# Half-height score matmuls in pairs: two heads' index and local-attention scores on the two row halves of the array

## The reference, cut to what matters

```
rel = relu(einsum('bqhd,bsd->bqhs', iq, ik))          # h = 8 heads, d = 64
score = einsum('bqhs,bqh->bqs', rel, iw) * idx_scale  # then the 128 largest
```

```
s = einsum('bnqhgd,bnkhd->bnhgqk', qb, kk)            # d = 64
s = where(mask, s + bias, -inf)
m = maximum(max(s), sink);  p = exp(s - m)
p = p / (sum(p) + exp(sink - m));  o = einsum('bnhgqk,bnkhd->bnqhgd', p, vv)
```

## Time and profile before

| | us |
|---|---|
| median of 3 runs (lowest, highest) | 1807.93 (1806.48, 1810.0) |
| span of the profiled execution, first to last instruction | 1813.4 |
| PE busy in it | 1714.0 (95%) |
| DVE, ACT, POOL busy | 790.4, 698.9, 643.8 |

### The profile page before, as it was taken

One profiled execution on the slowest core, in us unless ns is written; L12 is line 12 of the kernel. 1 busy time (PEld: TensorE's weight loads), 2 busy tenths in 40 slices (PEclk: granted clock), 3 DMA queues, 4 the chain that ended last, 5 costly groups with the idle time before them and its releaser, 6 DMA issues.

```text
span 1813.4 us, 22601 instructions
## 1 busy us (share of the span) xinstructions
PE 1714.0 (95%) x7710; PEld 1362.5 (75%) x7710; DVE 790.4 (44%) x1293; ACT 698.9 (39%) x1133; POOL 643.8 (36%) x269
## 2 busy tenths in 40 slices
PE   5999886999999999999999999889999999999997
PEld 3686663666678888888888788678986877887875
DVE  5486788444423321212123442534323464364464
ACT  4421455344433342323233332753354433243332
POOL 3232231122134444444444342024632344344342
PEclk8998997999999999999999999889999999999998
DMA  4121121111132222232322232013421223222221
GB/s 164 61 82 64 53 75 52 47 46 36 46 116 97 100 94 94 93 103 93 104 93 101 70 100 75 1 47 117 133 99 47 91 84 103 93 93 98 88 93 58
DMA packets 45147, 149.79 MB, mean 83 GB/s; under 512 B 4664, under 2 KB 7872, under 8 KB 45088
## 3 DMA queue, kind: packets, MB, share of 16 engines
q1 hardware_dynamic: 38016, 138.43, 22.9%
q10 hardware_dynamic: 7072, 10.57, 1.7%
HBM read 146.74 MB, written 2.11 MB: 82 GB/s over the span
## 4 chain that ended last, share of the span: by engine, by line
PE 76%; DVE 10%; ACT 7%; issue 5%; DMA 1%; ACTq 1%; DVEq 0%
PE job L304 21%; PE job L306 20%; PE job L305 20%; DVE arena L1317 5%; DVE arena L1320 2%; PE o L491 2%; ACT w_hi L791 2%; ACT arena L1265 2%; PE score L455 2%; PE turn L341 1%; PE score L388 1%; PE score L428 1%; PE score L712 1%; PE o L329 1%; PE job L744 1%
## 5 line engine op out<-in xcount | busy, mean ns | idle before, releaser
L274 POOL TENSOR_TENSOR w_lo<-w_raw,w_hi 128x1024 fp32r<-128x1024 f32 x264 | 643.1, 2439 | 1140.2 <-ACT w_hi L791 1139.8
L304 PE MATMUL job<-a_hi,w_hi 128*128 128x512 f32 (+1 forms) x1144 | 448.1, 392 | 23.7 <-POOL w_lo L274 12.1
L305 PE MATMUL job<-a_lo,w_hi 128*128 128x512 f32 (+1 forms) x1144 | 436.2, 381 | 0.0
L306 PE MATMUL job<-a_hi,w_lo 128*128 128x512 f32 (+1 forms) x1144 | 436.2, 381 | 0.0
L791 ACT ACTIVATE w_hi<-w_raw 128x1024 fp32r<-128x1024 f32 x264 | 275.2, 1050 | 283.3 <-PE job L306 279.8
L304 PE MATMUL job<-b_hi,w_hi 128*128 128x512 f32 x952 | 378.7, 398 | 1.1 <-DVE arena L1320 0.8
L306 PE MATMUL job<-b_hi,w_lo 128*128 128x512 f32 x952 | 371.2, 390 | 0.0
L305 PE MATMUL job<-b_lo,w_hi 128*128 128x512 f32 x952 | 370.7, 389 | 0.0
L304 PEld LDWEIGHTS job<-a_hi,w_hi 128*128 128x128 f32 x1144 | 218.4, 191 | 74.1 <-issue 18.1
L305 PEld LDWEIGHTS job<-a_lo,w_hi 128*128 128x128 f32 x1144 | 218.4, 191 | 41.6 <-issue 2.3
L306 PEld LDWEIGHTS job<-a_hi,w_lo 128*128 128x128 f32 x1144 | 217.9, 190 | 41.4
(11 more groups left out here) (245 smaller groups left out, 1399.3 us busy)
## 6 DMA issues: line engine op xcount, KB each, us to landing
w_raw<-w_all SPq DMA_DIRECT2D x264, 512.0 KB, 3.2
arena<-x_t ACTq DMA_DIRECT2D x8, 512.0 KB, 6.6
out_t<-arena ACTq DMA_DIRECT2D x8, 256.0 KB, 2.0
arena<-rg_w ACTq DMA_DIRECT2D x4, 256.0 KB, 2.7
arena<-row_table ACTq DMA_DIRECT2D x1, 1024.0 KB, 5.0
arena<-mem_t ACTq DMA_DIRECT2D x1, 1024.0 KB, 5.8
arena<-consts ACTq DMA_DIRECT2D x1, 384.0 KB, 4.1
cst<-consts ACTq DMA_DIRECT2D x1, 258.0 KB, 8.6
```

The lines of the kernel that those rows point to most:

```text
L274: nc.gpsimd.tensor_tensor(w_lo[:, sl], raw[:, sl], w_hi[:, sl].bitcast(F32), ALU.subtract).then_inc(s("lo_ready"), 1)
L304: mm(ps[:, 0:n], w_hi[:, sl, c], hi[:, kt, 0:n], start=kt == 0, stop=False)
L305: mm(ps[:, 0:n], w_hi[:, sl, c], lo[:, kt, 0:n], start=False, stop=False)
L306: ins = mm(ps[:, 0:n], w_lo[:, sl, c], hi[:, kt, 0:n], start=False, stop=kt == last)
```

## The change

The zero-padded keys go. `ik_rows` is one tile with the index key in partitions 0 to 63 and the same key in 64 to 127; `s_k` is one tile with the two local key heads one below the other. Each score matmul is issued on the 64 partitions of its own head only, with 64-row weights, which places it on the lower or the upper 64 rows of the array. The two memsets of the padded tiles, and one of two key copies, are gone. In the local-attention stage the blocks of heads 2t and 2t+1 are issued in turn: `swa_scores(0)` makes both heads before the first spreads, and the pair for heads 2t+2 and 2t+3 is issued after the turn of the odd head 2t+1, where before each head's scores came after the turn of the head two before it. The wait on `swa_s` is for both heads of the pair before.

```
-                mm(s_ps[n % 3][:, 0:P * (t + 1)], p1[:, J_IQ + h // 2, t * P:t * P + P],
-                   ikz[:, h % 2, 0:P * (t + 1)], start=True, stop=True).then_inc(s("idx_mm"), 1)
+                r = slice(64 * (h % 2), 64 * (h % 2) + 64)
+                mm(s_ps[n % 3][:, 0:P * (t + 1)], p1[r, J_IQ + h // 2, t * P:t * P + P],
+                   ik_rows[r, 0:P * (t + 1)], start=True, stop=True).then_inc(s("idx_mm"), 1)
...
-            def swa_scores(n):
-                t, half = n // 2, n % 2
-                if n >= 2:
-                    pe.wait_ge(s("swa_s"), n - 1)
+            def swa_block(n, b):
+                t, half = n // 2, n % 2
+                r = slice(64 * half, 64 * half + 64)
+                k0 = max(b - 1, 0) * P
+                c0 = b % 2 * 256 + (P if b == 0 else 0)
+                return mm(banks[half][b // 2][:, c0:b % 2 * 256 + 256], in2[r, 13 + t, b * P:b * P + P],
+                          s_k[r, k0:(b + 1) * P], start=True, stop=True)
+
+            def swa_scores(t):
+
+                if t >= 1:
+                    pe.wait_ge(s("swa_s"), 2 * t)
                 for b in range(QT):
-                    k0 = max(b - 1, 0) * P
-                    c0 = b % 2 * 256 + (P if b == 0 else 0)
-                    ins = mm(banks[n % 2][b // 2][:, c0:b % 2 * 256 + 256], in2[:, 13 + t, b * P:b * P + P],
-                             s_kz[:, half, k0:(b + 1) * P], start=True, stop=True)
+                    ins = swa_block(2 * t, b)
+                    if b == QT - 1:
+                        ins.then_inc(s("swa_mm"), 1)
+                    ins = swa_block(2 * t + 1, b)
                 ins.then_inc(s("swa_mm"), 1)
...
             go_spread(0)
             go_spread(1)
-            swa_scores(1)
...
-                if n < 6:
-                    swa_scores(n + 2)
+                if half == 1 and n < 6:
+                    swa_scores(t + 1)
                 pe.wait_ge(s("swa_pt"), 2 * n + 2)
...
-            did(v.memset(ikz, 0.0))
             dve.wait_ge(s("zeroed"), 1)
             norm_inverse(0)
...
             dve.wait_ge(s("go_ready"), 4)
-            did(v.memset(s_kz, 0.0))
-            settle()
-            did(v.tensor_copy(s_kz[0:64, 0, :], in2[0:64, 17, :]))
-            v.tensor_copy(s_kz[64:128, 1, :], in2[64:128, 17, :]).then_inc(s("swa_keys"), 1)
+            dve.wait_ge(s("job_taken"), J_IN2 + 18)
+            v.tensor_copy(s_k, in2[:, 17, :]).then_inc(s("swa_keys"), 1)
```

More of the change, by code:

```diff
@@ L160, in build @@
         keep = flat(tiles(28, 2)).bitcast(BF16).rearrange("p (t c) -> p t c", c=T)
-        ikz = tiles(30, 2)
+        ik_rows = arena[:, 30, :]
         rel = tiles(32, 2)
@@ L199, in build @@
         g_o = tiles(23, 4)
-        s_kz = tiles(2, 2)
+        s_k = arena[:, 2, :]
         s_vz = tiles(17, 2).rearrange("p g (t c) -> p g t c", c=P)
@@ L857, in _ @@
             act.wait_ge(s("ik_normed"), 1)
-            act.dma_start(ikz[64:128, 1, :], ikz[0:64, 0, :]).then_inc(s("ik_landed"), 16)
+            act.dma_start(ik_rows[64:128, :], ik_rows[0:64, :]).then_inc(s("ik_landed"), 16)
             split(8)
@@ L1401, in _ @@
             settle()
-            stt(ikz[0:64, 0, :], p1[0:64, 0, :], vcol("ikn")[0:64], t_ps[0][0:64, :]).then_inc(s("ik_normed"), 1)
+            stt(ik_rows[0:64, :], p1[0:64, 0, :], vcol("ikn")[0:64], t_ps[0][0:64, :]).then_inc(s("ik_normed"), 1)
             for k in (J_IQ + 3, J_K, J_K + 1):
```

## The result

The changed kernel takes 1825.03 us, the median of 4 runs (1820.01 to 1827.67), beside 1808.45 for the kernel before (4 runs, 1806.48 to 1810.0). The ratio is 1.0085 with a 95% interval of 1.0068 to 1.0102: 0.9% slower, 16.6 us. The profiled execution is the fastest of the four: 1820.01 us with a span of 1818.2 and a mean granted clock of 0.970, where the others had 0.963 or 0.964. Before, the profile had fallen on a long one. So the two profiles differ by 4.8 us and the medians by 16.6, and two profiles laid side by side do not add up to the result.

The account below looks back on a forecast made before the run. PE bounds the kernel (busy 1714 of 1813 us), but in local attention the steps on DVE and ACT do. +17.5 - 0.7 = +16.8 on 1807.9 gives 1824.7 us; range for 8 in 10: 1818.5 to 1831.

Parts of the forecast that it names:

- The late pairs: Local attention: scores for heads 2, 4 and 6 come after the odd head's turn, delaying their exponentials; +17.5 us.
- The clock in that term: Local attention: PE idles about 6 us; odd head's values product at half clock, even head's too, turn and scores at full.
- The ends: Local attention, odd head's exponentials to the next even head's: 10.72 us all at full clock, 14.44 all at half.
- Overlap: Local scores: the two row halves work at once, so a pair's even head is ready after 1.68 us.
- The rival without overlap: Local scores: halves run one after the other, even head's 1.08 us later four times; +4.3, 1829.0 us; chance 0.09.
- The tail: Local attention behind head 7's exponentials: still at half clock, 0, or up to 3 us gained if it is up.
- Memset: Front: without the 0.91 us memset DVE's step moves up and PE's turn comes earlier; 0.7 us gained.
- Index stage: Index scores: DVE's chain of additions sets the pace, so the gain is nothing, at most 0.1 us.
- The rival on the clock: Clock falls in the index stage, 1826.7 us, or also stays down all through local attention, 1833.4 us; chance 0.10.
- The sum: Whole kernel: +17.5 - 0.7 = +16.8 us on 1807.9, forecast 1824.7 us, 0.9% slower.
- the one of no difference: Local attention: later scores are covered after all, odd heads' distance being shortened by as much; no change; chance 0.02.
- the faster one: Local attention: four pairs save PE 1.5 us each, -6, with the memset -6.7: 1801.2 us; chance 0.02.

Follow-up runs that it names:

- the second profile: The kernel before, unchanged, run and profiled once more; 1808.63 us, ratio 1.0000.
- The order alone: The kernel before, full-height and padded, with local scores issued in pairs at the late places of the change; 1826.74 us, ratio 1.0099.
- the filling in the wrong place: The changed kernel plus six full-height products with unused results behind each late pair; 1830.6 us, ratio 1.0123.

## Why the prediction was right, step by step

*The late pairs (+17.5).* Right in mechanism and size. The three distances were forecast at 11.74, 12.20 and 12.20, 36.1 us in all, and came out at 12.65, 12.37 and 10.91, 35.9. From head 0's to head 7's exponentials the stage grew from 41.0 us (40.2 in the second profile) to 58.3, that is by 17.3 or 18.1. The order alone on full-height products gave 18.2 us in all. Moving the pair one head forward took 13 to 15 us off the changed kernel, and 8 off the full-height version.

*The clock in that term.* The values products of heads 1, 3 and 5 ran at half clock each time (3.36), as forecast. In the chain itself the forecast was right as an average, by parts that cancel, and that is in part luck. Only the second pair went as I had assumed, values product at half and turn at full clock; with the first pair even the turn ran at half clock (1.66), with the third the values product ran at full (1.83). The ends were 10.72 and 14.44: 10.91 came out at full clock, and 13.56 with the filling in the wrong place.

*Overlap.* Right, and better than the 2.3 us for 16 records that I named: 1.79. The rival without overlap is out. From turn to scores 0.86 us passed where 0.77 did, and the pair took 1.79 where one head took 1.68: 0.2 us for each pair. The drain that the Trainium skill names for a change of tiling mode (TensorEngine Tiling (Array Packing), Key Properties) would be among these. The head-by-head version at half height settles what it is not: there, with no second half at work, the same two steps take 0.86 (1163.89 to 1164.75) and 1.78 us. So the second half adds 0.01, and 0.2 us comes with half height itself; how much of that is a drain no run shows. Over three pairs it is 0.6 us.

*The tail (0, up to 3 gained).* Its size was off: from head 7's exponentials to the first job 10.93 us, where it was 14.70 and 12.43. The last two values products ran at full clock this time (1.83 each, at 1196.24 and 1199.52). The prediction also used two sizes for this gain, up to 3 us in the term and 1.7 at the low end of the sum.

*Memset (-0.7).* Its size was off. DVE's step moved up by 1.08 us, but then PE's own products at half clock ended the wait, and the turn gained 0.3 us on average. The turn stood at 35.63, not at 35.3 as I had said. I had seen the clock of these products nowhere in my rows.

*Index stage (0 to -0.1).* The size that I had furthest off: 1.0 us was gained. I said that PE leaves when DVE's chain lets it. The step that fails is that DVE alone set the pace: PE may be three products ahead, and before, it was not. At 512 columns it spent 0.86 us per product beside DVE's 0.84, and ACT's last five relus waited for PE. With overlap they wait mostly for DVE. That the last product now waits only for the relu three before it follows from the code and the rows, and I did not test it by itself. The rival on the clock showed in two of the eight profiles with half-height index scores, as 3 to 4 us at half clock within the stage; PE then left it 0.4 us later, no more.

*The sum.* +16.8 forecast, +16.6 measured. That it is this close is luck, for it is closer than its terms: the profiled tail, the index stage and the memset sum to 2 to 4 us more gain than I had put down (index 1.0, tail 1.5 to 3.8, memset 0.4 less), and the other three executions of the changed kernel took 5 to 7.7 us longer than the profiled one at a lower clock, which no profile resolves. Of the rivals, the one of no difference and the faster one are out by the time, and the one of no overlap by the 1.79 us.

*What the sum had at nothing* is a price that may hide in the result. The clock rival had half-height products lower the clock in the index stage, where two profiles show a delay of 0.4 us. In the local stage one head at a time, at the old places, they cost 5.4 us, with a clock of 0.74. That the overlap pays this back in the changed kernel is my reading of its being level with the full-height version of the same order; no run shows the two apart.

## What to carry to other kernels

In a stage that goes round several engines, find first which product some other engine waits for, and issue it early enough that the engine need not wait. What PE does not do meanwhile counts too: a full-height pair at the early place held PE for 3.04 us before a product that others waited for, and the kernel was 10.3 us slower than with one head at a time. Batching two heads is worth nothing if the batch starts where its last input is ready and its first consumer has long been idle. Products on part of the rows are cheap in time only when the other rows work at the same moment: alone they took as long as before, and in the local stage the granted clock fell with them (0.74); in the index stage it did so for a few microseconds in two profiles of eight, at no price in the median that can be told. Filling PE's pauses helped here only ahead of the product that sets the pace; filled elsewhere it moved the pause there.

## What the runs showed of the hardware that I had not expected

I had not reckoned with this when I predicted, beyond the 32-row spreads: a stream of products on 64 rows keeps 2.4 GHz if it begins there (25 us at 1.00) and does not bring it back if it begins at 1.2 (49 us at 0.50), with PE busy all of the time in both, each in one execution. Two streams on the two row halves, issued in turn with two records for each product, each ran at the rate of one alone, 0.43 us for a record of 512 fp32 columns, and together had the clock back. And the same kernel, profiled twice, spent 60.3 and 57.2 us in the same stage, with the same busy time on ACT (43.57 us both) and nearly the same on DVE (30.29 and 30.27), and granted clocks of 0.83 and 0.91.
